# Index stacks from two DMA queues, the top-k choice spread over attention, and two PSUM banks each for scores and transposes

## The chip, the cores and the metric

The kernel runs on 1 core of one Trainium2 chip. The metric is device time in microseconds (us), the median of several executions. TensorE (PE) multiplies, VectorE (DVE) and ScalarE (ACT) work element by element, SyncE (SP) issues the DMA transfers.

## The reference

A sequence of 512 tokens of width 1024 goes through two layers (an FFN, a mixer of four attention kinds, an FFN) and then through a second block (a state space part, a gated recurrence, an FFN), all in float32. The change touches the mixer, which runs once in each layer. Cut to what matters, one of its four kinds, for the queries of a block of 128:

```python
qi, wi = q_idx of the block (8 heads of 32), w_idx of the block
rel = relu(einsum('bqhd,bsd->bqhs', qi, k_idx))
score = einsum('bqh,bqhs->bqs', wi, rel)
score = where(k_pos[None, None, :] <= q_pos[None, :, None], score, NEG_INF)
_, idx = lax.top_k(score, 128)          # 128 keys of 512 for each query
p = masked_softmax(q . k[idx] * scale, idx <= q_pos)
out = p . v[idx]
```

The other kinds are dense causal attention with low-rank keys, attention with compressed, selected and windowed keys that are gated together, and stick-breaking attention, which has a cumulative sum of logarithms where the softmax would be.

## The kernel before

Features lie in partitions, tokens along a row (`[128, 512]` tiles `mix_h`), and float32 products are made of three passes over a high and a low part: `hi` is a rounded copy made by ACT (`L314` for weights), `lo` is the rest, made by DVE (`L318`), and PE runs hi by hi, hi by lo, lo by hi. Each stage is a `Phase`: all engines run their own written-out order with semaphores, and a barrier of all engines stands between two phases.

**The projection phase** (`mixer_front`). 20 slots `n`, one weight tile each: a `products` call of 24 matmuls of 512 columns, or, in the token slots 12 to 15, a `token_block`. Beside slot `n` each engine does what belongs there: DVE rotates features (`rope`), ACT and DVE split the index queries and keys (`index_hi`, `index_lo`), PE makes keys, values and compressed keys. The weight tile of slot `n + 2` is split during slot `n` (`ph.hi`, `ph.lo`); in the last two slots these calls split the first two tiles of the phase after the next, the mixer's output. For the index scores each of the 8 index heads needs a stack: four strips of 32 partitions, hi, lo, hi, lo, so that one matmul with the stacked keys does all passes. `stack(0)` and `stack(1)` on SP fill heads 0 to 3 and 4 to 7 with 16 transfers each (line 931), of 48 KB each. In the slots 16 to 19 (`stick_features`) PE puts 24 index score matmuls (line 1030) between the feature matmuls, 6 a slot; ACT takes them out of PSUM with a ReLU (`relus`, line 1147, tile `idx_rel`), and DVE adds them up in `idx_score` (lines 1223, 1227). `idx_rel` lies where the index queries were, so the first ReLU waits for both stacks (`istack_in1`).

**The attention phase** (`mixer_attention`). 20 groups (a kind and a query block) of 4 heads, 80 units `u`. A unit is a chain over three engines:

- PE `scores(u)` (lines 1370, 1371), then DVE `minimum(u)` (line 1560, the row minimum of the negated scores), then ACT `exponentials(u)` (line 1472), then PE `transposes(u)` (line 1380), then ACT `copy_transposed(u)` (line 1481), then PE `values(u)` (line 1391).

PSUM has 8 banks: scores turn through three (0 to 2), transposes have one (3), so `transposes(u)` waits for `copy_transposed(u - 1)`. PE's order in step `u` is `scores(u + 2)`, `transposes(u)`, `values(u - 1)`; ACT's is `exponentials(u + 1)`, `copy_transposed(u)`. Laid between are 16 stick-breaking pieces `s`, begun every 4.7 units: PE makes scores at step `u0`, ACT three operations at `u0 + 1`, DVE two at `u0 + 2`, PE the cumulative sum at `u0 + 3`, ACT and PE the rest. The top-k choice is 48 rounds on DVE, 16 for each of the query blocks 1 to 3: `largest` (line 1537, the 8 largest) and `take` (line 1544, removes them), one round in each of the units 0 to 47; `allow` makes the mask. Chosen keys are first used in units 48 (block 2), 64 (block 3) and 76 (block 1). In the units 0 to 11 ACT and DVE also split one of 12 `parts` each (queries and keys).

Of the kernel before, what the change touches and what calls it, by code (L numbers as in the profile page):

```python
# [7 lines left out]
F32 = mybir.dt.float32  # L8
# [6 lines left out]
P = 128  # L15
# [826 lines left out]
def mixer_front(c, m, l, following):  # L842
# [24 lines left out]
    index = (IDXK, IDXQ, IDXQ + 1)  # L867
# [18 lines left out]
    with ExitStack() as ctx:  # L886
# [5 lines left out]
        with nc.Block() as block:  # L892
            @block.sync
            def _(sp):
# [28 lines left out]
                def stack(i):  # L923

                    sp.wait_ge(ph["ilo_done"], i + 2)
                    t = IDXQ + i
                    hi, lo = m.split[t][0], m.split[t][1]
                    for h in range(4):
                        rows = slice(32 * h, 32 * h + 32)
                        for g in range(4):  # L930
                            sp.dma_start(stack_of[4 * i + h][32 * g:32 * g + 32].bitcast(F32), (hi, lo)[g % 2][rows, P:SEQ].bitcast(F32)).then_inc(ph[f"istack_in{i}"], 16)
# [3 lines left out]
                for n in range(slots):  # L935
# [31 lines left out]
                    if n == 14:  # L967
# [3 lines left out]

                        sp.wait_ge(ph["gelu_done"], 2)
                        stack(1)
# [6 lines left out]
            def _(pe):  # L980
# [89 lines left out]
                for n in range(2, slots):  # L1070
# [5 lines left out]
                    else:  # L1076
                        if n == TOK_AT + NTOK:
                            pe.wait_ge(ph["ilo_done"], 1)
                            pe.wait_ge(ph["cmp_done"], 2)
# [5 lines left out]
            def _(act):  # L1085
# [41 lines left out]
                def index_hi(i):  # L1127
                    if i == 0:
                        act.wait_ge(ph["idxk_in"], 64)
                    else:  # L1130
                        act.wait_ge(ph["rope_done"], parts[order.index(4 + i) + 1])
                    hi, _, src, _ = m.split[index[i]]
                    act.activation(hi, src, ACT.Copy).then_inc(ph["ihi_done"], 1)
                    if i == 0:
                        act.wait_ge(ph["copies_in"], 16 * 6)
                        act.activation(kstack[0:64], src[0:64], ACT.Copy).then_inc(ph["ihi_done"], 1)

                def relus(n):
                    for i in rels_of(n):
# [4 lines left out]
                        if i >= 3:  # L1144
# [6 lines left out]
                          11: lambda: (index_hi(2), gelus()), 12: compressed}  # L1151
                act.nop().then_inc(ph["bank_free"], 4)
                apply.act(act)
                for n in range(slots):
# [4 lines left out]
                    ph.hi(act, n // 4, n % 4, width(n + 2), last=n >= slots - 4)  # L1159
# [4 lines left out]
            def _(dve):  # L1164
# [36 lines left out]
                def index_lo(i):  # L1201
                    dve.wait_ge(ph["ihi_done"], i + 2)
                    hi, lo, src, _ = m.split[index[i]]
                    if i == 0:
# [27 lines left out]
                for n in range(slots):  # L1232
# [5 lines left out]
                    ph.lo(dve, n // 4, n % 4, width(n + 2), last=n >= slots - 4)  # L1238
# [10 lines left out]
                dve.wait_ge(ph["acc_done"], len(rels))  # L1249
# [1337 lines left out]
```

## Time and profile before

| | us |
|---|---|
| median of 3 executions | 3546.96 (3545.58, 3546.96, 3554.99) |
| the profiled execution, its own time | 3556.16 |
| its span, first to last instruction | 3554.3 |
| PE busy in it | 3322.8 (93%) |
| DVE busy | 1642.7 (46%) |
| ACT busy | 1413.4 (40%) |

Busy shares are of the span. The projection phase of layer 1 ends at 550.7 us of the span and its attention phase runs from 555.5 to 725.8; the attention of layer 2 runs from 1708.8 to 1873. The mean clock that TensorE was granted is 0.967 of full speed.

### The profile page before, as it was taken

What the parts mean: (1) busy time and instruction counts of PE and PEld (TensorE: products, weight loads), DVE (VectorE), ACT (ScalarE), POOL (GpSimd) and SP (SyncE); (2) the same over time, 40 slices, a digit from 0 to 9 for tenths busy, and PEclk for the clock granted to TensorE, in tenths of its full rate; (3) what the DMA queues carried; (4) which work ended last, traced back from release to release, by engine and by line L of the source; (5) the groups of instructions that cost most, each with busy time, mean ns of one, the idle gap of its engine ahead of it and who ended that gap; (6) DMA issues with size and microseconds to landing.
All of it is one profiled execution on the core that took longest, in us unless ns stands there. A gap on an engine that the chain in (4) does not pass through costs nothing. (4 is left out here: it accounts for less than half of the span.)

```text
span 3554.3 us, 41810 instructions
## 1 busy us (share of the span) xinstructions
PE 3322.8 (93%) x15368; PEld 2671.0 (75%) x15370; DVE 1642.7 (46%) x2465; ACT 1413.4 (40%) x2342; POOL 77.5 (2%) x52
## 2 busy tenths in 40 slices
PE   7999988989999999999898999979999899889998
PEld 5887776768888788777676888847777677768886
DVE  3333457753333433345865333366566346343333
ACT  4332436544322433243665332245555237233321
POOL 0001000010001000100001000100000000000000
PEclk9999998999999999999999999989999999999999
DMA  3232240012232233224001223211111222222231
GB/s 133 97 107 98 90 121 24 1 60 89 95 106 85 74 96 103 98 90 122 24 1 60 95 99 104 81 56 55 55 66 61 76 81 103 77 72 99 94 107 65
DMA packets 85880, 286.34 MB, mean 81 GB/s; under 512 B 15841, under 2 KB 19425, under 8 KB 85217
## 3 DMA queue, kind: packets, MB, share of 16 engines
q1 hardware_dynamic: 85728, 284.37, 24.3%
q8 instruction: 89, 1.46, 0.2%
q14 instruction: 63, 0.51, 0.0%
HBM read 269.12 MB, written 2.10 MB: 76 GB/s over the span
## 5 line engine op out<-in xcount | busy, mean ns | idle before, releaser
L318 DVE TENSOR_TENSOR wlo<-raw,whi 128x1024 fp32r<-128x1024 f32 (+3 forms) x464 | 609.3, 1313 | 989.0 <-ACT whi L314 988.8
L346 PE MATMUL ps<-xh,whi 128*128 128x512 f32 x2256 | 886.1, 393 | 16.7 <-DVE xl L2535 6.3
L347 PE MATMUL ps<-xl,whi 128*128 128x512 f32 x2256 | 880.1, 390 | 0.0
L348 PE MATMUL ps<-xh,wlo 128*128 128x512 f32 x2256 | 879.9, 390 | 0.0
L314 ACT ACTIVATE whi<-raw 128x1024 fp32r<-128x1024 f32 (+3 forms) x464 | 515.0, 1110 | 657.6 <-PE ps L348 614.3
L346 PEld LDWEIGHTS ps<-xh,whi 128*128 128x128 f32 x2256 | 425.2, 188 | 114.8 <-issue 25.1
L348 PEld LDWEIGHTS ps<-xh,wlo 128*128 128x128 f32 x2256 | 425.0, 188 | 88.7
L347 PEld LDWEIGHTS ps<-xl,whi 128*128 128x128 f32 x2256 | 425.1, 188 | 88.6 <-issue 1.7
L346 PE MATMUL ps<-ffn_hh,whi 128*128 128x512 f32 x880 | 347.2, 395 | 11.1 <-DVE ffn_hl L751 11.1
L347 PE MATMUL ps<-ffn_hl,whi 128*128 128x512 f32 x880 | 345.1, 392 | 0.0
L348 PE MATMUL ps<-ffn_hh,wlo 128*128 128x512 f32 x880 | 345.0, 392 | 0.0
L706 ACT ACTIVATE ffn_hh<-ffn_gate 128x512 f32 (+1 forms) x110 | 69.6, 633 | 512.0 <-DVE ffn_gate L749 512.0
L749 DVE TENSOR_TENSOR ffn_gate<-ffn_gate,ps 128x512 f32<-128x512 f32 x110 | 75.7, 688 | 282.6 <-PE ps L348 282.6
L346 PEld LDWEIGHTS ps<-ffn_hh,whi 128*128 128x128 f32 x880 | 166.8, 189 | 48.8 <-DVE ffn_hl L751 13.2
L347 PEld LDWEIGHTS ps<-ffn_hl,whi 128*128 128x128 f32 x880 | 166.8, 190 | 35.5 <-issue 1.0
L348 PEld LDWEIGHTS ps<-ffn_hh,wlo 128*128 128x128 f32 x880 | 166.7, 189 | 35.0
L1950 PE MATMUL ps<-xh,whi 128*128 128x512 f32 x384 | 159.9, 416 | 15.8 <-PEq L297 15.8
L702 ACT ACTIVATE ffn_gate<-ps 128x512 f32<-128x512 f32 x110 | 65.9, 599 | 257.1 <-PE ps L348 254.4
L1951 PE MATMUL ps<-xl,whi 128*128 128x512 f32 x384 | 152.8, 398 | 0.0
L1952 PE MATMUL ps<-xh,wlo 128*128 128x512 f32 x384 | 152.5, 397 | 0.0
L509 POOL TENSOR_TENSOR x<-x,mean_rest 128x512 f32<-128x512 f32 x48 | 77.3, 1644 | 2173.0 <-ACT mean_rest L473 2173.0
L751 DVE TENSOR_TENSOR ffn_hl<-ffn_gate,ffn_hh 128x512 f32 (+1 forms) x110 | 76.2, 693 | 98.8 <-ACT ffn_hh L706 98.8
(393 smaller groups left out, 4095.5 us busy)
## 6 DMA issues: line engine op xcount, KB each, us to landing
raw<-in_ffn_up SPq DMA_DIRECT2D x216, 512.0 KB, 3.5
raw<-in_ffn_down SPq DMA_DIRECT2D x80, 704.0 KB, 4.0
raw<-in_ssm_in SPq DMA_DIRECT2D x44, 512.0 KB, 3.5
raw<-in_mix_in SPq DMA_DIRECT2D x32, 512.0 KB, 3.6
raw<-in_lru_in SPq DMA_DIRECT2D x20, 512.0 KB, 3.6
raw<-in_mix_out SPq DMA_DIRECT2D x16, 512.0 KB, 3.7
raw<-in_ssm_out SPq DMA_DIRECT2D x16, 512.0 KB, 3.5
raw<-in_lru_out SPq DMA_DIRECT2D x8, 640.0 KB, 3.9
```

The lines of the kernel that those rows point to most:

```text
L314: act.activation(self.core.whi[:, u % HALF, 0:width], self.core.raw[:, u, 0:width], ACT.Copy).then_inc(sems["hi_done"], 1)
L318: dve.tensor_tensor(self.core.wlo[:, u % HALF, 0:width], self.core.raw[:, u, 0:width], self.core.whi[:, u % HALF, 0:width].bitcast(F32), A ...
L346: pe.matmul(out, c.whi[:, h, w], xh[:, k0 + k], start=first and k == 0, stop=False)
L347: pe.matmul(out, c.whi[:, h, w], xl[:, k0 + k], start=False, stop=False)
L348: mm = pe.matmul(out, c.wlo[:, h, w], xh[:, k0 + k], start=False, stop=last and k == nk - 1)
L509: pool.tensor_tensor(c.x[:, t], c.x[:, t], c.dneg[:], ALU.add).then_inc(ph["xc_done"], 1)
L706: act.activation(hh[:, p], gate[:, u // 2], ACT.Copy).then_inc(ph["hh_done"], 1)
L749: dve.tensor_tensor(gate[:, u // 2], gate[:, u // 2], c.ps[:, u], ALU.mult).then_inc(ph["prod_done"], 1)
L751: dve.tensor_tensor(hl[:, p], gate[:, u // 2], hh[:, p].bitcast(F32), ALU.subtract).then_inc(ph["hl_done"], 1)
L1950: pe.matmul(out, c.whi[:, h, w], c.xh[:, t], start=t == 0, stop=False)
L1951: pe.matmul(out, c.whi[:, h, w], c.xl[:, t], start=False, stop=False)
L1952: mm = pe.matmul(out, c.wlo[:, h, w], c.xh[:, t], start=False, stop=t == DT - 1)
```

## The change

In the projection phase the index order is queries first, keys last (`index`). A helper `stack_head(engine, h)` fills one head. Heads 0 to 3 are now issued by ACT from its own queue, in the slots 12, 13 (two) and 14; heads 6, 7, 4 and 5 by SP in the slots 12, 13 and 14, after smaller transfers that stood behind the stacks before. The two weight tiles of the output phase are no longer split in slots 18 and 19 but in units 34 and 36 of attention. The three additions of a mask to `idx_score` (`own`) go from the end of the projection to the units 3, 5 and 7.

In attention, scores have two banks (0, 1) and transposes two (2, 3): PE's step is `scores(u + 1)`, `transposes(u)`, `values(u - 1)`, and `transposes(u)` waits for `copy_transposed(u - 2)`. DVE's `minimum` moves along to `u + 1`. The 48 rounds go to the units 9 to 70, in three of four, in the order of blocks 2, 3, 1. Of the 12 parts the last five go to the units 20, 23, 26, 29 and 31.

```diff
@@ -864,7 +864,7 @@
-    index = (IDXK, IDXQ, IDXQ + 1)
+    index = (IDXQ, IDXQ + 1, IDXK)
...
@@ -877,6 +877,13 @@
+    def stack_head(engine, h):
+
+        hi, lo = m.split[IDXQ + h // 4][:2]
+        rows = slice(32 * (h % 4), 32 * (h % 4) + 32)
+        for g in range(4):
+            engine.dma_start(stack_of[h][32 * g:32 * g + 32].bitcast(F32), (hi, lo)[g % 2][rows, P:SEQ].bitcast(F32)).then_inc(ph[f"istack_in{h // 4}"], 16)
...
@@ -957,10 +958,6 @@
                     if n == 12:
 
-                        sp.wait_ge(ph["km_done"], HEADS)
-                        sp.wait_ge(ph["vm_done"], 2)
-                        stack(0)
-
                         sp.wait_ge(ph["rope_done"], parts[order.index(9) + 1])
                         for a in (0, 64):
                             sp.dma_start(m.h[a:a + 64, KWIN], m.h[64:P, KSLC]).then_inc(ph["kwin_in"], 16)
...
@@ -969,8 +966,15 @@
 
+                        stack((4, 5))
+                    if n == 12:
+
+                        sp.wait_ge(ph["ilo_done"], 2)
+                        stack((6,))
+                    if n == 13:
+
                         sp.wait_ge(ph["gelu_done"], 2)
-                        stack(1)
+                        stack((7,))
...
@@ -1125,15 +1129,21 @@
+                def stack(h):
+                    act.wait_ge(ph["ilo_done"], 1)
+                    act.wait_ge(ph["km_done"], HEADS)
+                    act.wait_ge(ph["vm_done"], 2)
+                    stack_head(act, h)
...
-                          11: lambda: (index_hi(2), gelus()), 12: compressed}
+                          11: lambda: (index_hi(2), gelus()), 12: lambda: (compressed(), stack(0)),
+                          13: lambda: (stack(1), stack(2)), 14: lambda: stack(3)}
...
@@ -1156,7 +1167,8 @@
                         act.activation(m.h[:, STORED[feature(n)]], c.ps[:, n % 4], ACT.Copy).then_inc(ph["bank_free"], 1)
-                    ph.hi(act, n // 4, n % 4, width(n + 2), last=n >= slots - 4)
+                    if n + 2 < slots:
+                        ph.hi(act, n // 4, n % 4, width(n + 2))
...
-                    ph.lo(dve, n // 4, n % 4, width(n + 2), last=n >= slots - 4)
+                    if n + 2 < slots:
+                        ph.lo(dve, n // 4, n % 4, width(n + 2))
...
-                dve.wait_ge(ph["acc_done"], len(rels))
-                for b in range(1, QB):
-                    own = m.picked[b][:, b * P:(b + 1) * P]
-                    dve.tensor_tensor(own, own, c.k["negd"], ALU.add).then_inc(ph["acc_done"], 1)
...
@@ -1307,18 +1316,21 @@
-    S_BANK, T_BANK, V_BANK, Z_BANK, Y_BANK = 0, 3, 4, 6, 7
+    S_BANK, T_BANK, V_BANK, Z_BANK, Y_BANK = 0, 2, 4, 6, 7
...
-    rounds = [(b, r) for b in range(1, QB) for r in range(TOPK // 8)]
+    chosen = (2, 3, 1)
+    rounds = [(b, r) for b in chosen for r in range(TOPK // 8)]
+    round_at = {9 + k * (n - 19) // (len(rounds) - 1): k for k in range(len(rounds))}
...
+    part_at = dict(zip((0, 1, 2, 3, 4, 5, 6, 20, 23, 26, 29, 31), range(len(parts))))
+    ahead_at = {34: 0, 36: 1}
...
-                    if u >= 3:
-
-                        pe.wait_ge(ph["exp_done"], u - 2)
+                    if u >= 2:
+
+                        pe.wait_ge(ph["exp_done"], u - 1)
...
                 def transposes(u):
                     x = units[u]
-                    if u >= 1:
-
-                        pe.wait_ge(ph["pt_done"], u)
+                    if u >= 2:
+
+                        pe.wait_ge(ph["pt_done"], u - 1)
                     pe.wait_ge(ph["exp_done"], u + 1)
                     for j in range(len(x["v"])):
-                        mm = pe.transpose(c.ps[:, T_BANK, j * P:(j + 1) * P], p_of(u)[:, j * P:(j + 1) * P], c.k["ident"])
+                        mm = pe.transpose(c.ps[:, T_BANK + u % 2, j * P:(j + 1) * P], p_of(u)[:, j * P:(j + 1) * P], c.k["ident"])
                     mm.then_inc(ph["t_done"], 1)
                 scores(0)
-                scores(1)
                 for u in range(n):
-                    if u + 2 < n:
-                        scores(u + 2)
+                    if u + 1 < n:
...
@@ -1518,36 +1531,37 @@
                         exponentials(u + 1)
                     for s in at_unit(u, 1):
                         stick_exp(s)
-                    if u < len(parts):
-                        hi(u)
+                    if u in part_at:
+                        hi(part_at[u])
+                    if u in ahead_at:
+                        ph.split_hi(act, c.sides[0], 0, ahead_at[u], D)
                     copy_transposed(u)
                     for s in at_unit(u, 1):
...
+                def own_block(b):
+                    own = picked[b][:, b * P:(b + 1) * P]
+                    dve.tensor_tensor(own, own, c.k["negd"], ALU.add).then_inc(ph["own_done"], 1)
+
+                def largest(k):
+                    b, r = rounds[k]
+                    dve.wait_ge(ph["own_done"], QB - 1)
+                    if k:
+
+                        dve.wait_ge(ph["took_done"], k)
+                    dve.max(top8, picked[b]).then_inc(ph["top_done"], 1)
+
+                def take(k):
+                    b, r = rounds[k]
+                    dve.wait_ge(ph["top_done"], k + 1)
+                    dve.match_replace(picked[b], top8, picked[b], TAKEN).then_inc(ph["took_done"], 1)
+
+                def allow(k):
+                    b, r = rounds[k]
+                    if r == TOPK // 8 - 1:
+                        dve.wait_ge(ph["took_done"], k + 1)
 
                         dve.tensor_scalar(allowed[b], picked[b], TAKEN, NEG, ALU.not_equal, ALU.mult).then_inc(ph["choice_done"], 1)
...
                 minimum(0)
-                minimum(1)
                 for u in range(n):
                     for s in at_unit(u, 2):
                         softplus(s)
-                    if u + 2 < n:
-                        minimum(u + 2)
+                    if u + 1 < n:
+                        minimum(u + 1)
...
                         dve.reciprocal(gate, gate).then_inc(ph["gates_done"], 1)
-                    largest()
+                    if u in (3, 5, 7):
+                        own_block((3, 5, 7).index(u) + 1)
+                    if u in round_at:
+                        largest(round_at[u])
...
-                    take()
-                    if u < len(parts):
-                        lo(u)
-                    allow()
+                    if u in round_at:
+                        take(round_at[u])
+                    if u in part_at:
+                        lo(part_at[u])
+                    if u in ahead_at:
+                        ph.split_lo(dve, c.sides[0], 0, ahead_at[u], D)
+                    if u in round_at:
+                        allow(round_at[u])
```

What ACT has in the token slots 12 to 15 of the projection. Before (`whi<-raw` is the split of a slot's weights, `cmp_v` the last of the compressed values, `idx_rel` the first ReLU):

```order
L314 ACTIVATE whi<-raw 128x936 [waits ring_b_raw_in2,ring_b_slot_used]
L1124 ACTIVATE cmp_k<-ps 128x31 [waits proj_pad_done,proj_kv_done]
L1125 ACTIVATE cmp_v<-ps 31x64
L314 ACTIVATE whi<-raw 128x936 [waits ring_b_raw_in3,ring_b_slot_used]
L314 ACTIVATE whi<-raw 128x1024 [waits ring_b_raw_in0,ring_b_slot_used]
L314 ACTIVATE whi<-raw 128x1024 [waits ring_b_raw_in1,ring_b_slot_used]
L1147 ACTIVATE idx_rel<-ps 128x256 [waits proj_istack_in1,proj_rel_done]
```

And now, from the same place (four `idx_stack` transfers a head):

```order
L1129 ACTIVATE cmp_v<-ps 31x64
L886 DMA idx_stack_1642<-index_hi 32x384 [waits proj_vm_done,proj_km_done,proj_ilo_done]
...
L314 ACTIVATE whi<-raw 128x936 [waits ring_b_raw_in3,ring_b_slot_used]
L886 DMA idx_stack_1642<-index_hi 32x384 [waits proj_vm_done,proj_km_done,proj_ilo_done]
...
L314 ACTIVATE whi<-raw 128x1024 [waits ring_b_raw_in0,ring_b_slot_used]
L886 DMA idx_stack_1642<-index_hi 32x384 [waits proj_vm_done,proj_km_done,proj_ilo_done]
...
L314 ACTIVATE whi<-raw 128x1024 [waits ring_b_raw_in1,ring_b_slot_used]
L1157 ACTIVATE idx_rel<-ps 128x256 [waits proj_istack_in1,proj_rel_done]
```

Four, eight and four transfers of the stack now stand ahead of the weight splits of slots 15, 16 and 17.

PE at the start of attention. Before (`mla_k,mla_q` with the mask `consts_bf` is a unit's scores, `att_p` its transposes, `att_pt` its values):

```order
L1370 MATMUL ps<-mla_k,mla_q 128x384
L1371 MATMUL ps<-consts_bf_57 128x128
L1380 MATMUL ps<-consts_sb,att_p 128x128 [waits att_exp_done]
L1380 MATMUL ps<-consts_sb,att_p 128x128 x2
L1370 MATMUL ps<-mla_k,mla_q 128x384 [waits att_exp_done]
L1371 MATMUL ps<-consts_bf_57 128x128
L1380 MATMUL ps<-consts_sb,att_p 128x128 [waits att_exp_done,att_pt_done]
L1380 MATMUL ps<-consts_sb,att_p 128x128 x2
L1391 MATMUL ps<-mla_v,att_pt 128x64 [waits att_pt_done]
```

Now:

```order
L1384 MATMUL ps<-mla_k,mla_q 128x384
L1385 MATMUL ps<-consts_bf_57 128x128
L1394 MATMUL ps<-consts_sb,att_p 128x128 [waits att_exp_done]
L1394 MATMUL ps<-consts_sb,att_p 128x128 x2
L1384 MATMUL ps<-mla_k,mla_q 128x384 [waits att_exp_done]
L1385 MATMUL ps<-consts_bf_57 128x128
L1394 MATMUL ps<-consts_sb,att_p 128x128 [waits att_exp_done]
L1394 MATMUL ps<-consts_sb,att_p 128x128 x2
L1405 MATMUL ps<-mla_v,att_pt 128x64 [waits att_pt_done]
```

The first rows shown are the scores of unit 2 before and of unit 1 now: one unit less lies between a unit's scores and its transposes, and the second transposes no longer wait for a copy (`att_pt_done`), while the values behind them do.

## Rows read from the trace of the kernel before

**Rows 1.** The page, part 1: busy us (share of the span), instructions

```profile
PE 3322.8 (93%) x15368; PEld 2671.0 (75%) x15370; DVE 1642.7 (46%) x2465; ACT 1413.4 (40%) x2342; POOL 77.5 (2%) x52
```

**Rows 2.** Waits from 500 to 556: who <- whom: us in total, times, longest

```profile
ACT idx_rel L1147 <- DMA idx_stack<-mix_h_split: 11.9, 1, 11.9
...
PE ps L1030 <- ACT idx_rel L1147: 8.8, 1, 8.8
```

**Rows 3.** Timeline of SP's queue: start us, us, engine line op, times

```profile
499.16 0.51 SPq L931 DMA_DIRECT2D idx_stack<-index_hi  x1
...
508.58 0.59 SPq L931 DMA_DIRECT2D idx_stack<-mix_h_split  x1
...
523.43 0.59 SPq L931 DMA_DIRECT2D idx_stack<-mix_h_split  x1
```

**Rows 4.** Timelines: first index score, first ReLU, and the restart in layer 2

```profile
513.47 0.28 PE L1030 MATMUL ps<-idx_kstack,idx_stack 128*128 128x256 f32 x1
...
525.42 1.92 ACT L1147 ACTIVATE idx_rel<-ps 128x256 f32<-128x256 f32 x5 [11.89 <-DMA idx_stack<-mix_h_split]
...
1678.87 0.69 PE L1030 MATMUL ps<-idx_kstack,idx_stack 128*128 128x384 f32 x1 [8.54 <-ACT idx_rel L1147]
```

**Rows 5.** Stretches: us; PE, PEld, DVE, ACT, POOL busy; PEclk, DMA share, GB/s

```profile
525.90:530.60 4.70, 4.70 (x11) 3.75 (x12) 2.90 (x6) 2.04 (x5) 0.00 (x0) 0.50 0.53 200
...
555.50:560.60 5.10, 5.07 (x12) 2.72 (x13) 1.81 (x4) 3.27 (x7) 0.00 (x0) 0.50 0.00 0
```

**Rows 6.** Transfers from 498 to 526: times, KB each, median us to landing

```profile
idx_stack<-mix_h_split SPq DMA_DIRECT2D x16, 48.0 KB, 2.0
```

**Rows 7.** Timeline of ACT in the token slots

```profile
497.47 0.20 ACT L1125 ACTIVATE cmp_v<-ps 31x64 f32<-31x64 f32 x1
502.24 0.99 ACT L314 ACTIVATE whi<-raw 128x936 fp32r<-128x936 f32 x1 [4.57 <-PE ps L1044]
507.36 1.06 ACT L314 ACTIVATE whi<-raw 128x1024 fp32r<-128x1024 f32 x1 [4.13 <-PE ps L1044]
```

**Rows 8.** Timelines: end of the projection, start of attention

```profile
550.69 0.60 ACT L1158 ACTIVATE mix_h<-ps 128x512 f32<-128x512 f32 x1 [0.76 <-PE ps L1060]
...
553.40 0.69 DVE L1252 TENSOR_TENSOR idx_score<-idx_score,consts_sb 128x128 f32<-128x128 f32 x3
...
555.53 0.98 PE L1370 MATMUL ps<-mla_k,mla_q 96*128 96x384 f32 x1 [4.88 <-PEq L297]
```

**Rows 9.** Waits in the attention of layer 2, 1709 to 1872

```profile
ACT att_p L1472 <- DVE att_least L1560: 19.4, 24, 2.0
...
PE ps L1380 <- ACT att_pt L1481: 11.0, 16, 1.7
...
PE ps L1416 <- DVE sb_sp L1615: 3.1, 4, 1.7
```

**Rows 10.** Stretches of the attention of layer 1, columns as above

```profile
560.60:583.50 22.90, 18.26 (x115) 13.53 (x114) 22.21 (x63) 18.62 (x51) 0.00 (x0) 0.95 0.20 46
...
634.00:667.00 33.00, 27.78 (x199) 22.77 (x199) 32.04 (x89) 18.18 (x63) 0.00 (x0) 1.00 0.00 1
...
670.50:718.00 47.50, 45.92 (x335) 39.02 (x335) 20.42 (x60) 31.03 (x104) 0.00 (x0) 1.00 0.00 1
```

**Rows 11.** Timelines around unit 8: its exponentials, copy 7, transposes 8

```profile
574.11 0.69 ACT L1472 ACTIVATE att_p<-ps,att_least 128x512 f32<-128x512 f32 x1 [1.35 <-DVE att_least L1560]
...
576.08 0.28 ACT L1481 ACTIVATE att_pt<-ps 128x128 f32<-128x128 f32 x1
...
576.40 0.66 PE L1380 MATMUL ps<-consts_sb,att_p 128*128 128x128 f32 x4 [1.27 <-ACT att_pt L1481]
```

**Rows 12.** Groups by form, 555 to 726: times | busy us, mean ns | idle before

```profile
L1537 DVE MAX8 idx_top<-idx_score 128x8 f32<-128x256 f32 x16 | 6.7, 418 | 0.1
...
L1472 ACT ACTIVATE att_p<-ps,att_least 128x128 f32<-128x128 f32 x16 | 5.9, 367 | 4.9 <-DVE att_least L1560 4.8
...
L1560 DVE TENSOR_REDUCE att_least<-ps 128x1 f32<-128x128 f32 x16 | 4.6, 286 | 5.5 <-PE ps L1371 5.5
```

More of the change, by code:

```diff
@@ L922, in _, with stack @@
                 sp.dma_start(c1[:], d["cmp1"][l].rearrange("p (j n) -> p j n", j=16)).then_inc(ph["c1_in"], 16)
[L923 to L931, printed above, removed]
+                def stack(heads):
+                    for h in heads:
+                        stack_head(sp, h)
                 load(4)
@@ L1201, in index_lo @@
                 def index_lo(i):
-                    dve.wait_ge(ph["ihi_done"], i + 2)
+                    dve.wait_ge(ph["ihi_done"], i + 1)
                     hi, lo, src, _ = m.split[index[i]]
-                    if i == 0:
+                    if index[i] == IDXK:
                         hi, lo, src = hi[64:P], kstack[64:P], src[64:P]
@@ L1315, in mixer_attention @@
     n = len(units)
-    rounds = [(b, r) for b in range(1, QB) for r in range(TOPK // 8)]
+    chosen = (2, 3, 1)
+    rounds = [(b, r) for b in chosen for r in range(TOPK // 8)]
+    round_at = {9 + k * (n - 19) // (len(rounds) - 1): k for k in range(len(rounds))}
+    done_at = {b: max(u for u, k in round_at.items() if rounds[k][0] == b) for b in chosen}
     first_unit = {}
@@ L1320, in mixer_attention @@
         first_unit.setdefault(g["mixer"], HEADS * k)
-    assert all(first_unit[2, b] >= b * (TOPK // 8) + 4 for b in range(1, QB)), "one round a unit"
+    assert len(round_at) == len(rounds) and all(first_unit[2, b] >= done_at[b] + 4 for b in chosen), "the choice comes in time"
     shortened = lambda x: x["width"] < P
@@ L1362, in scores @@
                         pe.wait_ge(ph["dsaq_in"], 64)
-                    for b in range(1, QB):
+                    for b in chosen:
                         if u == first_unit[2, b]:
-                            pe.wait_ge(ph["choice_done"], b)
-                    s = c.ps[:, S_BANK + u % 3]
+                            pe.wait_ge(ph["choice_done"], chosen.index(b) + 1)
+                    s = c.ps[:, S_BANK + u % 2]
                     mw = x["mask"].shape[-1]
@@ L1433, in _ @@
                 scores(0)
-                scores(1)
                 for u in range(n):
-                    if u + 2 < n:
-                        scores(u + 2)
+                    if u + 1 < n:
+                        scores(u + 1)
                     transposes(u)
@@ L1528, in _ @@
             def _(dve):
-                took, allows = [0], [0]
-                def largest():
-                    if took[0] < len(rounds):
-                        b, r = rounds[took[0]]
-                        if took[0]:
-                            dve.wait_ge(ph["took_done"], took[0])
-                        dve.max(top8, picked[b]).then_inc(ph["top_done"], 1)
-                def take():
-                    if took[0] < len(rounds):
-                        b, r = rounds[took[0]]
-                        took[0] += 1
-                        dve.wait_ge(ph["top_done"], took[0])
-                        dve.match_replace(picked[b], top8, picked[b], TAKEN).then_inc(ph["took_done"], 1)
-                def allow():
-                    if took[0] and rounds[took[0] - 1][1] == TOPK // 8 - 1 and took[0] // (TOPK // 8) > allows[0]:
-                        b = rounds[took[0] - 1][0]
-                        allows[0] += 1
-                        dve.wait_ge(ph["took_done"], took[0])
+                def own_block(b):
[15 more added lines that the diff above has]
+                        dve.wait_ge(ph["took_done"], k + 1)
                         dve.tensor_scalar(allowed[b], picked[b], TAKEN, NEG, ALU.not_equal, ALU.mult).then_inc(ph["choice_done"], 1)
```

18 lines of the change are left out of this document (9 added, 9 removed).

## The prediction

> **What bounds the kernel now.** I read the page first: PE is busy 93% of the span [rows 1], so a change can only win where PE waits or where its clock is low, and only in the mixer, twice. So I looked for PE's waits there, stage by stage.
>
> The projection has one long one. The waits show PE idle for 8.8 us, until an ACT instruction that itself waited 11.9 us for a transfer of the index stack [rows 2]. The timeline shows why. SP issues a stack's 16 transfers one behind the other, the first set from 499.16 to 508.58: 9.42 us over 15 steps, 0.63 us each. The last transfer of the second set is issued at 523.43 [rows 3] and lands about 2.0 us later [rows 6], and at 525.42 the first ReLU runs [rows 4]. PE read the first stack at 513.47 [rows 4]; it has four banks for index scores and then stands. The queue's issue is the limit here. In layer 2 the same wait is 8.54 us [rows 4]. The stall costs again afterwards: the 4.7 us of matmuls behind it run at a granted clock of 0.50, the 1.2 GHz level [rows 5].
>
> The second place is the border to attention. The projection's last ACT work that stays starts at 550.69, but DVE's three mask additions begin at 553.40, after a weight split, and PE starts attention at 555.53 after 4.88 us without work [rows 8], at a clock of 0.50 [rows 5].
>
> In attention PE is idle less than it seems. In layer 2 it waits 11.0 us in 16 waits for ACT's copies, with the transposes, and 3.1 us for the stick-breaking pieces [rows 9]. Where DVE has rounds and splits it is the one with no time left: 22.21 us busy of 22.90 and 32.04 of 33, with PE at 18.26 and 27.78; where it has neither, PE is busy 45.92 of 47.5 [rows 10].
>
> **The change part by part.**
>
> *Stacks, per layer.* ACT can begin heads 0 to 3 behind the row at 497.47 [rows 7]: four transfers at 0.63 us end at 500.2. The next eight follow the split that begins at 502.24 and takes 0.99 us: 503.3 to 508.3. The split of slot 16's weights began at 507.36 [rows 7] and is now 0.9 us late, its DVE half too; both are done about 510.6, before the index stage opens near 513, so this costs nothing; if an issue took ACT 1.2 us, it would be done some 5 us later and PE would wait for 2 to 3. The last four end about 511.9 and land 2.0 us later, at 513.9. PE loads the first of them as weights some 0.2 us ahead of its row at 513.47, at 513.2: a new wait of 0.7 us. Nothing else of ACT is queued behind them but splits. SP has half the heads left: from 499.2, 16 transfers (10.1 us), two shorter copies and a third (1.8), two weight loads (0.9), and about 1 us of waiting for a load's release: 513.0, landing at 515.0. PE's four banks carry it to about 516.7, so the ReLUs come in time. ACT as an issuer is not in the trace. Bounds: nothing for ACT (then 0 instead of 0.7) to double the SP row, 1.26 us (then 5 us). I take SP's own 0.63, the nearest row. The Trainium skill, DMA: Bandwidth & Descriptors, Issuing engines are not separate DMA queues, says that transfers of all issuers share 16 engines, and a second issuer saves only the sequencer's time. The rows agree that this is the part that limits here, so by it the sum is the same.
>
> The wait goes from 8.8 to 0.7: 8.1 us. Half of the 4.7 us at half clock comes back, 2.3, if the clock no longer falls there: 10.4, and 10.1 in layer 2. **10.3.**
>
> *End of the projection, per layer.* The three additions and two splits leave. What ends last is then ACT's copy, 550.69 + 0.60 = 551.29, where before DVE ended at about 554.1. The barrier's 1.4 us after it stays. **2.8.** The additions are hidden in units 3, 5, 7, which lose nine rounds; the splits come back in units 34 and 36, 1.2 us of DVE and 1.1 of ACT each, in a stretch where DVE has no slack; I count these in the attention term.
>
> *Clock at the start of attention.* PE's gap becomes 2.1 us. If the clock does not fall, half of 5.1 us is won [rows 5], if it does, nothing. I take the middle, **1.2.**
>
> *Attention, per layer.* Three effects.
>
> (a) Two transpose banks. The row of unit 8 shows what it can give: the transposes waited 1.27 us for copy 7, from 576.08 [rows 11]. But `values(7)` stands right behind them and waits for the same copy. So a wait of this kind gives back at most the transposes' own time, 0.1 to 0.45 us, and not itself: 16 of them about 4.5 us, not 11.0.
>
> (b) Spread rounds. The two stretches where DVE has no slack hold 4.6 and 5.2 us of idle PE [rows 10]. With three rounds in four units instead of four, and none before unit 9, I expect about half to go, 5. The rounds of block 1 (MAX8 0.42 us [rows 12] and a replacement as long) land where DVE was half idle, hidden.
>
> (c) One unit less ahead. From `scores(u + 1)` on, minimum and exponentials must be through before `transposes(u + 1)`, and PE has only `transposes(u)`, `values(u - 1)` and `scores(u + 2)` to cover them; before, one unit more. For units 128 wide the chain is 0.29 + 0.37 us [rows 12] and I allow 0.3 for reading the row sum and handing over, 1.0; PE's cover is 0.7 when no stick piece lies there. 32 units are narrow: up to 0.3 each, 10 us in all. When DVE or ACT is inside a stick piece or a round, the next minimum starts late and the stall is longer: with 16 pieces at up to 0.8 us another 13. Most narrow units lie beside wide ones or stick work, which cover: I take 10 of the 23.
>
> Sum: -4.5 - 5 + 10, about **0**, with -14 (all of 11.0 and 3.1) and +23 as the ends.
>
> Per layer 10.3 + 2.8 + 1.2 + 0 = 14.3, for two layers 28.6. The profiled execution's own time is 3556.16, so 3527.6 by it. It lies 9.2 above the median; on the median 3546.96 - 28.6 = **3518**.
>
> **Rivals.** *The spread wins in attention.* DVE's rows [rows 10] speak for it: rounds and splits fill it exactly where PE idles. 8 us a layer, most of (b) and (a): 3518 - 16 = 3502.
>
> *Attention loses some.* The nearest row for (c) is 45.92 of 47.5 [rows 10], a stretch with no slack to lose. 8 us a layer: 3534.
>
> *The two queues take turns.* If a transfer is prepared for one queue at a time, the work stays serial: 32 transfers and the rest, 20.2 + 2.7 us from 497.7, end at 520.6 and land at 522.6, instead of 525.4. 2.8 us instead of 10.3, the clock still falls: with 2.8 and 1.2 it is 6.8 a layer, 3533. For it: the SP rows stand at 0.63 us however busy the 16 DMA engines are; against it, nothing. The Trainium skill, Perfetto Trace Analysis, DMA Instruction — HWDGE (DVE, Sync), describes this: the block that generates descriptors is shared by sequencers and locked for one at a time. No row here has two issuers. By its rule the time is the 3533 above.
>
> *Slower: the shorter lead decides.* In the same place as (c), but without cover: the exponentials of every unit end after PE is ready for them. It must cost more than 14.3 a layer to undo the gain, 0.18 us for each of 80 units; measurably slower is 19.6, or 0.25. At (c)'s full 23 and no (a) or (b) the time is 3518 + 46 = 3564. ACT already waits 19.4 us for minima with a lead of two [rows 9], which speaks for it; that wide units and stick pieces cover more than the chain speaks against.
>
> **How the numbers follow.** The forecast as summed has 0.40, attention winning 0.20, attention losing 0.15, turns 0.17, the shorter lead 0.06, and 0.02 is left. The range from 3498 to 3540 takes in the first four. A measurement tells 0.3%, 10.6 us, from no change: below 3536.3 is faster. The two cases at 3533 and 3534 lie close to it, and I give a third of each to no change: faster 0.81, same 0.13, slower 0.06.
>
> **What would show it.** Stacks: PE's wait before the ReLU at 1 us or less; transfers of ACT and SP overlapping, 0.6 us each; granted clock 1.0 in slots 16 and 17. If they take turns: rows of 1.2 us while both issue. Border: PE's gap near 2.1 us. Attention: `transposes` no longer waiting for copies but for exponentials, `values` taking over part of the old waits, narrow units each with a small wait, DVE without a full stretch; its length against the 170 and 164 us of before. The prediction is wrong if ACT's issues hold up a weight split, so that PE waits ahead of slot 16, or if attention grows by over 14 us a layer.

## The result, and the profile after

The changed kernel takes 3584.62 us (median of 4 runs, 3582.84 to 3587.56) against 3546.61 beside it: a ratio of 1.0103, 95% interval 1.0085 to 1.012. It is 38 us slower, where 28.6 less was forecast. The range, 3498 to 3540, did not hold it. The profiled execution has a span of 3581.5 us against 3554.3.

I cut both spans at the first scores and the last values of each attention. Stretches of the changed kernel: us; PE, PEld, DVE, ACT, POOL busy (instructions); PEclk, DMA share, GB/s.

```profile
539.77:733.29 193.52, 167.56 (x987) 130.45 (x989) 124.70 (x349) 104.63 (x324) 0.00 (x0) 0.87 0.03 6
733.29:1703.89 970.60, 941.35 (x4042) 755.61 (x4042) 399.84 (x472) 342.92 (x461) 38.65 (x24) 0.99 0.30 94
1703.89:1899.12 195.23, 173.13 (x988) 137.27 (x989) 125.00 (x349) 105.47 (x324) 0.00 (x0) 0.83 0.03 6
1899.12:3581.50 1682.38, 1558.06 (x7160) 1253.26 (x7159) 772.11 (x1026) 671.03 (x981) 25.33 (x16) 0.96 0.25 80
```

The two attentions of the kernel before, same columns:

```profile
555.53:725.14 169.61, 155.31 (x988) 127.12 (x989) 120.23 (x344) 102.08 (x322) 0.00 (x0) 0.89 0.03 7
1708.85:1871.93 163.08, 148.31 (x988) 120.89 (x989) 120.01 (x344) 101.74 (x322) 0.00 (x0) 0.94 0.03 8
```

Attention starts 555.53 - 539.77 = 15.8 us earlier in layer 1, and the way from its end to the second attention is (1708.85 - 725.14) - 970.60 = 13.1 shorter. The attentions themselves are 23.9 and 32.1 longer. -15.8 + 23.9 - 13.1 + 32.1 = 27.1, the whole difference of the spans; behind them nothing has moved. (The medians differ by 38: the profiled execution of the kernel before is 9 us above its median. In experiment 1, whose code ahead of each attention is that of before, the way from the first attention to the second takes 979.3 us, 4.4 less than the 983.7 of before, so single terms of this sum are good to some us.) So the stretches ahead of attention got shorter by about what was forecast, and attention lost twice that.

**Ahead of attention.** The timeline of the two queues, which answers to [rows 3]:

```profile
503.12 0.52 ACTq L886 DMA_DIRECT2D idx_stack<-index_hi  x1
503.16 0.62 SPq L886 DMA_DIRECT2D idx_stack<-index_hi  x1
503.67 0.61 ACTq L886 DMA_DIRECT2D idx_stack<-mix_h_split  x1
503.82 0.75 SPq L886 DMA_DIRECT2D idx_stack<-mix_h_split  x1
504.31 0.63 ACTq L886 DMA_DIRECT2D idx_stack<-index_hi  x1
504.61 0.61 SPq L886 DMA_DIRECT2D idx_stack<-index_hi  x1
```

Both queues issue at once, each at its own pace; there are no rows of 1.2 us. The first index score and the first ReLU, against 513.47 and 525.42 in [rows 4]:

```profile
511.83 0.28 PE L1034 MATMUL ps<-idx_kstack,idx_stack 128*128 128x256 f32 x1
...
514.88 0.77 ACT L1157 ACTIVATE idx_rel<-ps 128x256 f32<-128x256 f32 x2 [3.12 <-DMA idx_stack<-mix_h_split]
```

PE's wait of 8.8 us [rows 2] is gone; the longest that is left there is 0.39 for a copy of DVE. The granted clock, 0.50 behind that wait in [rows 5], stays up (columns as above):

```profile
511.00:539.00 28.00, 26.66 (x120) 21.67 (x120) 18.26 (x30) 15.93 (x31) 0.00 (x0) 1.00 0.27 81
```

The transfers land later than in [rows 6] (issues: times, KB each, median us to landing), while two queues fill the 16 DMA engines (share 0.70 from 495 to 511, where before it was 0.42 from 499 to 509):

```profile
idx_stack<-index_hi ACTq DMA_DIRECT2D x16, 48.0 KB, 2.8
idx_stack<-mix_h_split ACTq DMA_DIRECT2D x16, 48.0 KB, 3.4
idx_stack<-index_hi SPq DMA_DIRECT2D x16, 48.0 KB, 3.2
```

**In attention.** The waits of layer 1, 539.77 to 733.29 (who <- whom: us in total, times, longest):

```profile
ACT att_p L1485 <- DVE att_least L1574: 55.5, 56, 2.4
...
PEld ps L1394 <- issue: 27.1, 36, 1.8
PE ps L1394 <- ACT att_p L1485: 15.7, 22, 1.7
...
PE ps L1405 <- ACT att_pt L1494: 5.2, 13, 1.1
PE ps L1394 <- ACT att_p_cmp L1485: 4.1, 6, 1.7
```

ACT now waits for minima in 56 units, not 24 as in [rows 9], and PE's transposes wait for exponentials, not for the copy before. How such a stall is made shows in the timeline around a compressed unit of block 1, 31 columns wide:

```profile
638.42 0.21 PE L1385 MATMUL ps<-consts_bf 128*128 128x32 bf16 x1
...
639.63 0.68 DVE L1559 MATCH_REPLACE8 idx_score<-idx_top,idx_score 128x512 f32<-128x512 f32 x1
640.22 0.68 DVE L1623 SCALAR_TENSOR_TENSOR sb_sp<-ps,sb_e 128x512 f32<-128x512 f32 x1
640.23 0.33 PE L1385 MATMUL ps<-consts_bf 128*128 128x128 bf16 x1
640.82 0.18 DVE L1574 TENSOR_REDUCE att_least<-ps 128x1 f32<-128x32 f32 x1
...
641.03 0.29 ACT L1485 ACTIVATE att_p_cmp<-ps,att_least 128x31 f32<-128x31 f32 x1 [1.57 <-DVE att_least L1574]
641.21 0.19 ACT L1485 ACTIVATION_READ_ACCUMULATOR att_p_cmp<-ps,att_least 128x1 f32 x1
...
641.55 0.45 PE L1394 MATMUL ps<-consts_sb,att_p_cmp 128*128 128x128 f32 x1 [0.99 <-ACT att_p_cmp L1485]
```

The unit's scores end at 638.63. DVE then finishes a group, replaces the eight largest of a round and forms a stick piece, and comes to the minimum, 0.18 us long, at 640.82. With one unit of lead PE has by then done the next scores (to 640.56) and stands 0.99 us. But PE's idle time is the smaller part of the loss. In layer 1 it goes from 169.61 - 155.31 = 14.3 to 26.0 us, +11.7, and PE's busy time goes up by 12.3 with the same matmuls; in layer 2 the two go up by 7.3 and 24.8. The clock column says much of the why: 0.87 and 0.83, where it was 0.89 and 0.94. Summed over the stretches whose clock is 0.50, PE is busy for 48.2 and 63.8 us in the two attentions, where it was 36.6 and 20.0. If work at that level takes twice its time, an estimate, half of the difference is its price: 5.8 us in layer 1 and 21.9 in layer 2. The other 6.5 and 2.9 us of busy time have no cause shown.

### The profile page after: what moved, and what is told of

The parts are those of the page before. It is cut to its first block and busy times, and to the rows that moved or that the text cites. A ratio compares the mean times of both kernels' runs of the same rounds, so it can differ in the third digit from the quotient of the medians.

```text
span 3581.5 us, 41954 instructions
## 1 busy us (share of the span) xinstructions
PE 3351.1 (94%) x15368; PEld 2683.7 (75%) x15370; DVE 1646.4 (46%) x2465; ACT 1416.3 (40%) x2342; POOL 77.5 (2%) x52
## 5 line engine op out<-in xcount | busy, mean ns | idle before, releaser
L346 PE MATMUL ps<-ffn_hh,whi 128*128 128x512 f32 x880 | 346.4, 394 | 11.1 <-DVE ffn_hl L751 11.1
L347 PEld LDWEIGHTS ps<-ffn_hl,whi 128*128 128x128 f32 x880 | 166.3, 189 | 35.6 <-issue 1.0
```

Source lines behind the costliest of these rows:

```text
L346: pe.matmul(out, c.whi[:, h, w], xh[:, k0 + k], start=first and k == 0, stop=False)
L347: pe.matmul(out, c.whi[:, h, w], xl[:, k0 + k], start=False, stop=False)
```

## Experiments

Times are medians; each ratio is to the kernel before, run on the same chip.

**1. The order alone.** Three score banks and one transpose bank stay, nothing else of the change is in.

```diff
-                scores(1)
                 for u in range(n):
-                    if u + 2 < n:
-                        scores(u + 2)
+                    if u + 1 < n:
+                        scores(u + 1)
...
-                    if u + 2 < n:
-                        minimum(u + 2)
+                    if u + 1 < n:
+                        minimum(u + 1)
```

> The kernel before, with its three score banks and one transpose bank, its projection and its rounds; only the order changes: the scores and the minimum of unit u+1 ahead of the transposes of unit u, where they were those of u+2. Theory A, the shorter lead decides: attention grows from 170.3 and 164.2 us by 25 to 32 us in each layer, as in the changed kernel (194.7 and 195), PE's waits for exponentials appear, and the time is 3595 to 3610. Theory B, the work spread over attention costs the time (rounds, splits, additions): nothing of it is here, 3540 to 3555. Theory C, the number of score banks decides, not the order: the third bank is still there, so 3540 to 3560.

3621.73 us, ratio 1.0214 (1.0195 to 1.0232): 74 us slower, more than the changed kernel. Its attentions:

```profile
555.08:755.64 200.56, 169.58 (x988) 133.03 (x989) 121.71 (x344) 103.86 (x322) 0.00 (x0) 0.84 0.03 6
...
1734.96:1934.53 199.57, 170.78 (x989) 135.57 (x989) 121.70 (x344) 103.79 (x322) 0.00 (x0) 0.83 0.03 6
```

Theories B (what is spread) and C (the number of score banks) fall: neither is changed in this kernel. A had the sign, and was too small by 12 us. One sign of A came otherwise than expected. PE's transposes wait for copies here, not for exponentials:

```profile
PE ps L1380 <- ACT att_pt L1480: 30.2, 37, 2.7
```

With one transpose bank `transposes(u)` still needs `copy_transposed(u - 1)`, which stands behind `exponentials(u)` in ACT's order, so late exponentials make the copy late.

**2. Banks and order**, still without stacks and spreading.

```diff
-    S_BANK, T_BANK, V_BANK, Z_BANK, Y_BANK = 0, 3, 4, 6, 7
+    S_BANK, T_BANK, V_BANK, Z_BANK, Y_BANK = 0, 2, 4, 6, 7
...
-                    if u >= 1:
-                        pe.wait_ge(ph["pt_done"], u)
+                    if u >= 2:
+                        pe.wait_ge(ph["pt_done"], u - 1)
```

> The kernel before with the changed kernel's banks and order (two banks for scores, two for transposes, one unit ahead), without its stacks and without anything spread. Theory A: as the kernel before with the order alone, less up to 4.5 us a layer for the second transpose bank: 3586 to 3610. Theory B: 3540 to 3555. Theory C: 3595 to 3610 here, and no loss in the kernel that has the order alone.

3611.92 us, 1.0176 (1.0159 to 1.0193). With the order already changed, moving one bank from scores to transposes gives 9.8 us back, 4.9 a layer; all else is the order's.

**3. The changed kernel with the old banks and order.** The edits of experiments 1 and 2, undone in the changed kernel.

```diff
-    S_BANK, T_BANK, V_BANK, Z_BANK, Y_BANK = 0, 2, 4, 6, 7
+    S_BANK, T_BANK, V_BANK, Z_BANK, Y_BANK = 0, 3, 4, 6, 7
...
-                    if u + 1 < n:
-                        scores(u + 1)
+                    if u + 2 < n:
+                        scores(u + 2)
```

> The changed kernel (stacks from two queues, splits and additions and rounds spread) with the banks and the order of before: three score banks, one transpose bank, two units ahead. Theory A: attention is back at about 170 and 164 us, and the 15.8 us a layer won ahead of it stay: 3546.6 - 31.6 = 3515, and 5 to 10 us less where the spread rounds free DVE: 3505 to 3520. Theory B: attention stays near 190 us: 3560 to 3585. Theory C: as A.

3509.44 us, 0.9892 (0.9876 to 0.9909): 38 us faster than the kernel before, 75 faster than the changed one. (The 15.8 us of the expectation are layer 1's; ahead of layer 2's attention it was 13.1.) Attention:

```profile
542.01:698.72 156.71, 143.52 (x988) 116.78 (x989) 122.85 (x349) 102.91 (x324) 0.00 (x0) 0.96 0.03 8
1668.29:1825.08 156.79, 143.61 (x989) 116.76 (x989) 122.94 (x349) 102.92 (x324) 0.00 (x0) 0.96 0.03 8
```

It is shorter even than before, by 12.9 and 6.3 us, of which PE's idle time gives 1.1 and 1.6 and its busy time, at a clock of 0.96, the rest. One trace of each is a weak basis for such a difference: experiment 5 has the attention code of before, and there the two take 161.2 and 166.3 us at 0.95 and 0.92, where before's take 169.6 and 163.1 at 0.89 and 0.94.

**4. The changed banks, two units ahead.** The order alone undone; the scores of u+2 wait for the exponentials of u.

```diff
+                scores(1)
                 for u in range(n):
-                    if u + 1 < n:
-                        scores(u + 1)
+                    if u + 2 < n:
+                        scores(u + 2)
```

(and the same for the minimum.)

> The changed kernel with its two and two banks, but scores and minimum two units ahead in the order, as before. The scores of unit u+2 then need the bank of unit u, so they wait for its exponentials, as the transposes behind them do; but between the scores of a unit and the first wait for its exponentials PE has one unit's transposes and values more than now. Theory A: most of the loss goes: 3515 to 3540. Theory B: no change, 3575 to 3590. Theory C: the wait only moves from the transposes to the scores: 3565 to 3590.

3509.36 us, 0.9894 (0.9877 to 0.991), the same as experiment 3. Theory A holds, and C falls a second time: with two score banks the loss is gone, because the wait for the same exponentials now comes a unit's transposes and values later. The waits of layer 1:

```profile
ACT att_p L1486 <- DVE att_least L1575: 17.0, 20, 3.0
...
PE ps L1384 <- ACT att_p L1486: 6.3, 10, 1.7
```

17.0 us in 20, where the changed kernel had 55.5 in 56.

**5. Stacks alone**: two queues and the order of the index splits, in the kernel before.

```diff
+                def stack(h):
+                    act.wait_ge(ph["ilo_done"], 1)
+                    act.wait_ge(ph["km_done"], HEADS)
+                    act.wait_ge(ph["vm_done"], 2)
+                    stack_head(act, h)
```

> The kernel before with one part of the change: the index stacks' transfers from two queues, with the order of the index splits that goes with it. Additions, last weight splits, rounds, banks and order stay as before. By the prediction's terms: 10.3 us a layer, 3527. If the stall's end also leaves the clock high into attention, up to 7 us more a layer: 3513. If the stacks were part of the loss (landing of 3.2 us where it was 2.0): 3540 or more.

3527.42 us, 0.9943 (0.9922 to 0.9964): 21.6 us for the two layers, where 20.6 was forecast. The interval is some 7 us wide to either side, so the agreement is closer than the runs can tell. Attention of layer 1 starts at 545.27, 10.3 us earlier.

**6. Spreading alone**: the rounds and weight splits of attention at the changed kernel's units.

```diff
+    round_at = {9 + k * (n - 19) // (len(rounds) - 1): k for k in range(len(rounds))}
+    part_at = dict(zip((0, 1, 2, 3, 4, 5, 6, 20, 23, 26, 29, 31), range(len(parts))))
```

> The kernel before with rounds of the choice and weight splits of attention spread over its units, three score banks and two units ahead as before, projection as before. By the prediction's term (b): 5 us a layer, 3538. Theory clock (each wait taken from PE in attention also raises its granted clock, so that it counts about three times): 8 to 15 us a layer, 3518 to 3531. If spreading costs: 3550 or more.

3535.45 us, 0.996 (0.9945 to 0.9974): 6.8 us a layer, between term (b) and the other theory. PE's idle time there is only 2.0 and 2.6 us less than before; the clock is 0.94 and 0.96.

**7. Stacks and spreading.** Experiment 3 with the additions and last splits still at the projection's end.

```diff
-                    if u in ahead_at:
-                        ph.split_hi(act, c.sides[0], 0, ahead_at[u], D)
...
-                    if u in (3, 5, 7):
-                        own_block((3, 5, 7).index(u) + 1)
```

> Stacks and spread together, banks and order as before, but the three additions and the last two weight splits stay at the projection's end. Against the changed kernel with the old banks and order (3509.4) it lacks only their move. By the prediction's term, 2.8 us a layer: 3515. If the clock at the start of attention depends on the gap there, 3515 to 3525; if the move is worth nothing, 3509.

3511.95 us, 0.989 (0.9869 to 0.991). Experiment 3 has only their move more and is 2.5 us faster, less than the runs can tell: the four times here go from 3507.5 to 3516.6. In the profiles PE's gap is 4.88 us here and 2.06 there, and the attention of layer 1 starts at 544.56 and 542.01.

**8 and 9. Work put into the waits.** In the changed kernel PE does matmuls that nothing reads: before the transposes of 22 units (experiment 8), then half as many again of them, and some before the values of 11 units (experiment 9).

```diff
+                    for _ in range(filled.get(u, 0)):
+                        pe.matmul(c.ps[:, T_BANK + u % 2, 0:P], c.kb["nident"], c.kb["negd"], start=True, stop=True)
                     pe.wait_ge(ph["exp_done"], u + 1)
```

> The changed kernel with work added: in the 22 units of each layer where its transposes waited for the exponentials, PE does 3 to 12 matmuls of 128 columns before that wait, about as long as the wait, into the transpose bank that it is about to overwrite; nothing reads them. Theory clock (two thirds of the loss is the lower granted clock that the waits bring, one third the waits): the clock in attention rises from 0.85 to over 0.92 and the time falls, 3530 to 3565, although there is more work. Rival (the waits are the loss, and the clock has another cause): clock stays at 0.85 and the fillers cost what sticks out of the waits, 3585 to 3605.

3572.16 us, 1.0063 (1.0046 to 1.008). Outside both ranges: 12.5 us faster than the changed kernel, with more work, but the clock rose only to 0.89 and 0.88 from 0.87 and 0.83.

Experiment 9 has larger numbers in the table and this ahead of the values:

```diff
+                    for _ in range(filled_values.get(u, 0)):
+                        pe.matmul(c.ps[:, S_BANK + (u + 1) % 2, 0:P], c.kb["nident"], c.kb["negd"], start=True, stop=True)
                     pe.wait_ge(ph["pt_done"], u + 1)
```

> As the filled kernel (3572.2, clock in attention 0.89 and 0.88), with more of the added matmuls: half as many again before the waits for exponentials (5 to 18 each), and 2 to 11 before the 11 longest waits of the values for a copy, into a score bank that is free then. Theory clock: the clock rises further, over 0.92, and the time falls again, 3545 to 3568. Rival (filling gave what it could; the low stretches have another cause): clock 0.85 to 0.89, and what sticks out costs 1 to 5 us a layer, 3574 to 3585.

3567.43 us, 1.0058 (1.0041 to 1.0074), with 234 matmuls added to each layer:

```profile
542.34:729.59 187.25, 174.22 (x1222) 138.36 (x1223) 124.76 (x349) 104.72 (x324) 0.00 (x0) 0.92 0.03 7
...
1699.70:1886.42 186.72, 173.51 (x1222) 138.67 (x1223) 124.67 (x349) 104.53 (x324) 0.00 (x0) 0.92 0.03 7
```

PE's busy time in the stretches at 0.50 goes from 48.2 and 63.8 us to 30.0 and 29.7. I know of no reason but the clock for which added work would shorten the time. What the added matmuls take where they stick out of a wait keeps it from going further.

**10. The minimum ahead of the stick piece** on DVE, in the changed kernel.

```diff
+                    if u + 1 < n:
+                        minimum(u + 1)
                     for s in at_unit(u, 2):
                         softplus(s)
-                    if u + 1 < n:
-                        minimum(u + 1)
```

> The changed kernel with one pair of calls exchanged on DVE: the minimum of unit u+1 ahead of the raw stick-breaking piece, not behind it. If the longest stalls come from minima that stand behind such pieces (16 a layer, 0.3 to 0.7 us each), they get shorter by the piece: 3 to 8 us a layer, 3568 to 3580. If the piece then waits behind the minimum for scores, and the stick chain is late instead: 3584 to 3600.

3568.5 us, 1.0061 (1.0044 to 1.0077): 16 us faster for two layers, the most that was expected. So the stall read at 640.82 is no single case. Its attentions:

```profile
542.14:730.97 188.83, 172.46 (x989) 136.99 (x989) 126.54 (x349) 104.02 (x324) 0.00 (x0) 0.83 0.03 7
...
1699.91:1888.40 188.49, 170.03 (x988) 134.84 (x989) 126.69 (x349) 103.97 (x324) 0.00 (x0) 0.85 0.03 7
```

PE's idle time falls from 26.0 to 16.4 us in layer 1, and yet the clock there is lower than in the changed kernel, 0.83 to 0.87. Less idle time in sum is not by itself a higher clock.

**11 and 12. Copies ahead of weight splits** on ACT, in experiments 3 and 4.

```diff
+                    copy_transposed(u)
                     if u in part_at:
                         hi(part_at[u])
                     if u in ahead_at:
                         ph.split_hi(act, c.sides[0], 0, ahead_at[u], D)
-                    copy_transposed(u)
```

> The changed kernel with the old banks and order (3509.4), and in addition ACT's weight splits behind the copy of their unit, not ahead of it (14 places a layer, 0.6 to 1.3 us each). PE still waits 9.6 us a layer for copies there. If half of that is copies behind splits: 3 to 5 us a layer, 3500 to 3504. If they only change places with the next exponentials: 3507 to 3512.

3511.71 us, 0.9892 (0.9875 to 0.9908): nothing won, the second reading. In both attentions of its trace PE is idle for 11.7 and 11.5 us, 1.5 less than in experiment 3, at a clock of 0.92, where that had 0.96.

> The changed kernel's two and two banks with two units ahead (3509.4), and ACT's weight splits behind the copy of their unit. PE waits for exponentials there, 7.9 us in 15 waits, and 0.4 for copies. A split moved behind the copy is then ahead of the next stick piece and exponentials as before, so little is won: 3506 to 3511; with a split no longer between a copy and its values, at best 3503.

3519.97 us, 0.9931 (0.9915 to 0.9948): a miss, some 10 us slower than experiment 4. PE's idle time in the attention of layer 1 is the same (11.1 us, 10.9 there) and its clock is not, 0.90 to 0.95:

```profile
540.09:705.69 165.60, 154.49 (x988) 124.83 (x989) 123.89 (x349) 103.45 (x324) 0.00 (x0) 0.90 0.03 8
...
1674.51:1832.50 157.99, 144.11 (x989) 117.09 (x989) 123.46 (x349) 102.79 (x324) 0.00 (x0) 0.97 0.03 8
```

Layer 2 of the same execution runs the same order of instructions at 0.97, with more idle time, 13.9 us, and is 7.6 us shorter.

## Why the prediction was wrong

**Stacks.** Right: 10.3 a layer forecast, 21.6 for both measured, by 0.60 to 0.61 us (median) for each issue on either queue at once, and a clock of 1.00 behind it. The rival of queues taking turns is refuted: its rows of 1.2 us are not there, the longest is 0.75. The reading given for it, SP's rows at 0.63 us however busy the DMA engines, overlooked a row of 1.78 us at 514.00 in the trace of before. The Trainium skill, Perfetto Trace Analysis, DMA Instruction — HWDGE (DVE, Sync), has one block that serves the sequencers one at a time. The rows at 503.12 to 504.61 show two issuers with rows of 0.6 us side by side, so at this rate its turns cost nothing that can be seen; a lock much shorter than a row they can't exclude.

**End of the projection and clock at its border.** PE's gap is 2.06 us, as forecast (2.1). What of the 5.6 for both layers reaches the time the runs can't tell: the medians differ by 2.5, within the noise. The 1.2 for the clock did not come: in experiment 4 PE's first microseconds of attention (540.4 to 547.3) are at 0.51. In the changed kernel the clock is back at 543.8, and falls again at 550.7.

**Attention (a), second transpose bank.** Forecast -4.5 a layer, measured -4.9 with one unit ahead. With two ahead it is worth nothing (experiments 3 and 4).

**Attention (b), spreading.** Forecast -5, measured -6.8 with two units ahead; with one ahead most of it is missing (see what stays open).

**Attention (c), one unit less ahead.** This is the step that failed. The text put it at "up to 0.3 each, 10 us in all", added "another 13" for stick pieces and rounds, and took "10 of the 23". The order alone costs 74 us, 37 a layer. Two things were wrong in it. The stall was too small: PE's idle time rises by 16.7 and 14.0 us (experiment 1 against before), where 10 were taken. "Most narrow units lie beside wide ones or stick work, which cover" was wrong on the stick work: what covers PE delays the minimum on DVE, and experiment 10 gets 8 us a layer back by one exchange. And the larger part was not in the sum at all: PE's busy time rises by 14.3 and 22.5 us, with the clock down from 0.89 and 0.94 to 0.84 and 0.83. PE is busy at 0.50 for 59.1 and 63.0 us, where before had 36.6 and 20.0; by the estimate above that is 11.3 and 21.5 of the rise. The text priced a clock at the two borders, by [rows 5], and took every stall inside attention at its own length. One place shows it, the stretch after the first weight splits; the changed kernel:

```profile
547.25:554.08 6.83, 4.98 (x27) 3.96 (x27) 3.43 (x8) 4.56 (x11) 0.00 (x0) 0.75 0.17 38
554.08:567.73 13.65, 13.50 (x43) 8.71 (x43) 5.90 (x16) 6.68 (x24) 0.00 (x0) 0.50 0.09 20
```

and experiment 4:

```profile
547.25:554.08 6.83, 6.45 (x48) 5.51 (x48) 5.39 (x15) 6.68 (x23) 0.00 (x0) 0.99 0.20 48
554.08:567.73 13.65, 13.65 (x100) 11.01 (x98) 10.48 (x28) 9.04 (x29) 0.00 (x0) 1.00 0.07 17
```

The PE rows of the changed kernel with a wait, from 547 on:

```profile
547.03 0.88 PE L1405 MATMUL ps<-mla_v,att_pt 128*128 128x64 f32 x6 [0.29 <-ACT att_pt L1494]
...
548.64 0.52 PE L1394 MATMUL ps<-consts_sb,att_p 128*128 128x128 f32 x3 [0.39 <-ACT att_p L1485]
550.23 1.17 PE L1405 MATMUL ps<-mla_v,att_pt 128*128 128x64 f32 x6 [1.07 <-ACT att_pt L1494]
```

PE stands for 0.29, 0.39 and 1.07 us, 1.75 in all; at 550.7 the granted clock falls, and PE then works nearly without a pause at the 1.2 GHz level until 567.7. In experiment 4 it pauses for 0.38 us between 547.25 and 554.08 and works on at 2.4. The 13.5 us of work in the second stretch would have taken half at the higher level: by this estimate some 6.7 us lost there, behind 1.75 us of pauses.

**The rival.** "Slower: the shorter lead decides" named the mechanism, with 0.25 us a unit as the point where it is measurable; it had a chance of 0.06. Experiment 1 measured 37 us for 80 units, 0.46 each. Its sign stood in [rows 9], where ACT waited 19.4 us for minima with a lead of two, and was given too little weight: a chain that is already late in 24 units had no unit to give away. The rival's price, 23 a layer, left out the clock too. The text's own sign of being wrong, attention longer by over 14 us a layer, came true in both layers (23.9 and 32.1).

**What stays open.** That the waits lower the clock is shown by experiments 8 and 9 as a direction, not as an amount: filling them brings 0.92, not 0.96. Experiment 11 and layer 1 of experiments 10 and 12 have a lower clock with less or the same idle time in sum. And each clock column is that of one execution: the same attention code had 0.89 and 0.94 once, 0.95 and 0.92 another time (before and experiment 5). Which pauses count is not settled here. The measured parts (-21.6, -13.6, +64.1, -2.5) add to +26.4, the whole change gives +38. Nearly all of the 11.6 between them lies between the order and the rest. With two units ahead stacks, spreading and the move bring 38.4 us (experiment 3), as their parts add to 37.7; with one unit ahead they bring 27.3 (experiment 2 to the changed kernel). And it is the spreading that fails there: the attentions take 195.8 and 195.6 us in experiment 2, without it, and 193.5 and 195.2 in the changed kernel, with it. Why, no run says. Three score banks together with two transpose banks, two units ahead, were not tried: they need nine banks, or the two value banks in one, which DVE would then have to read while PE writes it; no run here shows how that goes.

## What to carry to other kernels

In a ring of engines, count how many units each hand-over has before it is waited for, and look at how often the chain is already late before taking one away; the number of buffers mattered less here than the place of the producer in the program's order. A stall of PE is to be priced with the clock that follows it: in experiment 1 about as much again, 30.7 us of idle time and by estimate 32.8 of clock. When one change has parts that can be undone alone, time them alone: this one holds 38 us of gain under 75 of loss, and the kernel that keeps the gain (experiments 3 and 4, 3509.4 us) beats both.

## What the runs showed of the hardware

Eight issues on ACT's queue, 500.55 to 505.60, cost ACT next to nothing: the first begins while the weight split of 500.46 (0.99 us) is still running, and the next split comes 5.24 us after it, at 505.70, where [rows 7] have 5.12 without them. Two queues at once keep their 0.60 us per issue of 48 KB (median; longest 0.75), but a transfer's landing goes from a median of 1.9 to 2.0 us to 2.8 to 3.4. And matmuls that nobody needs, placed where PE would have waited, made the program 17 us faster.
